# Four gate tiles of the delta projection computed inside the delta rule's first chunk

## The chip, the cores and the metric

The kernel runs on one core of a Trainium2 chip. The metric is the device time of one execution in microseconds (us); the kernel before takes 1758.41 us, the median of 3 runs (1757.74 to 1760.31). The engines of the core are TensorE (PE in the rows, its weight loads PEld), VectorE (DVE), ScalarE (ACT), GpSimd (POOL) and the queue that issues the transfers (SP). Each works through its own list of instructions in order, and they wait for one another by semaphores.

## What is computed

The reference is two transformer blocks on 256 tokens of width 1024: in the first, two kinds of attention and a layer of 16384 small experts; in the second, banded attention and then a gated delta rule, the mixer at which the change is made. 16 meta tokens stand in front there, so that it sees L = 272 tokens.

```
u = rms_norm(h, norm_w) @ w_in
qkv, z, b, a = split(u, [4096, 4096 + 2048, ... + 16])
qkv = silu(causal_depthwise_conv(qkv, conv_w))
q, k, v = split(qkv)                      # q, k l2-normed
beta = sigmoid(b)
g = -exp(a_log) * softplus(a + dt_bias)
o = chunked_gated_delta_rule(q, k, v, beta, g)
o = rms_norm(o, o_norm_w) * silu(z)
return o @ w_out
```

The gate z is needed only at the last step, when an output is multiplied by silu(z).

## The kernel before, in words

All weights come through a ring of four tiles of 128x1024 (512 KB each), loaded by SP in the order in which they are used. A weight tile is split in two: ScalarE rounds it to its high part (`make_high`, L177), and VectorE or GpSimd subtracts that from the tile for the low part (`make_low`, L189). Both parts have two buffers. TensorE multiplies a tile of the projection in 24 matmuls of 272 columns: 8 of the high part with the rounded input, 8 of the high part with the rest of the input, 8 of the low part (`tile_T`, L229 and L233). `tile_piece` (L272) does the same 24 matmuls in pieces, and is used so far to fill the attention stage.

**The projection** (`delta_in_stage`) has 49 tiles: 32 for the convolutions (c0 to c31; q, k, v), one for beta and the decays, 16 for the gate (z0 to z15). `mix_order` writes their order: a pair of convolution tiles and a gate tile in turn, with the tile of beta and the decays in the place of the first gate tile and one gate tile left over at the end. A convolution costs VectorE one multiplication and three multiply-adds (L1981, L1984) and ScalarE a Silu (L2047, or L2055 and L2056) and for q and k a square (L2051); it has three PSUM banks and two buffers of results, so that convolution i waits for the Silu of convolution i-2. A gate tile costs ScalarE one Silu out of PSUM (L2070). The low parts of the tiles with odd numbers are made by GpSimd from the third tile on, those with even ones by VectorE. Between the tiles stand matmuls that collect sums of squares (L1935, "gather") and spread the norms back (L1943, "spread", taken by VectorE in L2635, or L2640 and L2641). Steps on the decays are pinned to tile numbers t: at t=5 VectorE makes the doubled decays (L2009 to L2014), and at t=6 TensorE transposes them (L1960).

**The delta rule** (`delta_stage`) works through 5 chunks; chunk 0 holds the 16 meta tokens and has 3 levels of the inverse, the others have 5. Ahead of chunk 0 stand the decay sums and key products (`key_sums`, L2155 and L2157), the transposes of the keys (`turn_keys`, L2176) and values (`turn_values`, L2182), and `turn_m` (L2188), which needs the decays' exponentials and products of ScalarE and VectorE (L2563, L2396). Then each level has, for both halves b of the heads: `square` on TensorE (L2202), a copy by ScalarE (`take_power`, L2579), the product `grow` on TensorE (L2216), and an add on VectorE (`add_inverse`, L2427). The functions `beside` put the work of the next and the last chunk between these steps. A chunk ends with `solve` (L2225, L2230). PSUM banks 6 and 7 are unused in chunk 0. `store_out` multiplies the outputs of a chunk by the gate.

Both stages are blocks of their own: all engines meet between them. The four first tiles of the output weights (`dn_out`) are loaded at the start of the delta rule and split at its end.

Of the kernel before, what the change touches and what calls it, by code (L numbers as in the profile page):

```python
# [10 lines left out]
ACT = mybir.ActivationFunctionType  # L11
# [34 lines left out]
PAD = NCH * CH - L  # L46

# [47 lines left out]
def plan(k):  # L95
# [38 lines left out]
    for n in range(len(r.slots)):  # L134
        k.split.append(None if n in plain else n - sum(q < n for q in plain))
        engine = "gpsimd" if k.tiles["dn_in"] + AHEAD <= n < k.tiles["dn_out"] and n % 2 else "vector"
        made[engine] += n not in plain
        k.low_nth.append((engine, made[engine]))
# [1730 lines left out]
def mix_order():  # L1869


    out, z = [], 0
    for pair in range(DNK + DNV // 2):
        out += [("conv", 2 * pair), ("conv", 2 * pair + 1)]
        if pair == 0:
            out.append(("ba", 0))
        else:
            out.append(("z", z))
            z += 1
    return out + [("z", i) for i in range(z, DNV)]  # L1880


def delta_in_stage(k, unit, norm):
# [4 lines left out]
    first, order = k.tiles["dn_in"], mix_order()  # L1888
# [24 lines left out]
    with nc.Block() as block:  # L1913
# [58 lines left out]
        def _(dve):  # L1972
# [21 lines left out]
            for t in range(count):  # L1994
# [10 lines left out]
                if t + AHEAD < count and k.low_nth[first + t + AHEAD][0] == "vector":  # L2005
                    make_low(dve, k, first + t + AHEAD)
# [35 lines left out]
        def _(act):  # L2042
# [17 lines left out]
            for t in range(count + 1):  # L2060
                if t + AHEAD < count:
                    make_high(act, k, first + t + AHEAD)
# [32 lines left out]
def delta_stage(k):  # L2095
# [17 lines left out]
    rooted, normed, stored, chain, mean = k.start("d_rooted", "d_normed", "d_stored", "d_chain", "d_mean")  # L2113
    H = 4
# [25 lines left out]
    with nc.Block() as block:  # L2140
# [6 lines left out]
        def _(pe):  # L2147
            def key_sums(c):
# [155 lines left out]
            def beside(c, l, b):  # L2304

                if c + 1 < NCH:
# [24 lines left out]
            turn_keys(0, 0)  # L2331
            turn_m(0)
            turn_keys(0, 1)
# [27 lines left out]
        def _(dve):  # L2361
# [95 lines left out]
            def store_out(c):  # L2457
                dve.wait_ge(*oturn.at(c))
                for b in range(2):
# [36 lines left out]
            products(0)  # L2496
            key_rows(0, 1)
            value_rows(0, 0)
            value_rows(0, 1)
            for c in range(NCH):  # L2500
                first_inverse(c)
                if c + 1 < NCH:
                    spread_gates(c + 1)
                for l in range(1, levels(c) + 1):
                    for b in range(2):
                        beside(c, l, b)
                        add_inverse(c, l, b)
                if c:
# [41 lines left out]
        def _(act):  # L2550
# [30 lines left out]

            decays(0)
            take_turned(0)
            for c in range(NCH):
                for l in range(1, levels(c) + 1):
                    for b in range(2):
                        take_power(c, l, b)
                        if c + 1 < NCH and (l, b) == (2, 0):
# [500 lines left out]
```

## Time and profile before

| | us |
|---|---|
| median of 3 runs | 1758.41 |
| the profiled execution | 1757.97 |
| its span | 1756.2 |
| TensorE busy | 1665.5 (95%) |
| VectorE busy | 1188.5 (68%) |
| ScalarE busy | 896.0 (51%) |
| GpSimd busy | 71.1 (4%) |

A row of a timeline merges instructions of one line that follow each other: when the first started, how long they took to the end of the last, how many, and in brackets how long the engine had stood idle before and what ended that. In the trace a float32 matmul outside the tiles counts twice (the 16 of `square` as 32). The time from the start of one row to the start of the next is the pitch. The granted clock is that of TensorE, 1.00 for 2.4 GHz and 0.50 for 1.2 GHz.

### The profile page before, as it was taken

To read this page: it belongs to the slowest core of one execution; us is meant where nothing else is said; L and a number is where in the kernel's file an instruction comes from. 1 tells how busy PE (TensorE), PEld (TensorE's weight loads), DVE (VectorE), ACT (ScalarE), POOL (GpSimd) and SP (SyncE) were. 2 spreads that over 40 slices of the span, in tenths; PEclk is the share of its full clock that TensorE was granted. 3 is DMA by queue.
4 is the path that set the end of the run, shared out by engine and by line. 5 is a ranking of instruction groups with operands and counts; after the bars stand their busy time and mean duration, and the time that the engine had idled before them with its cause. 6 is when DMAs were issued, how large, how long until landed. Compare 5 with 4: busy or idle time off the path is not lost. (4 is left out here: it accounts for less than half of the span.)

```text
span 1756.2 us, 34029 instructions
## 1 busy us (share of the span) xinstructions
PE 1665.5 (95%) x13058; PEld 1469.2 (84%) x13058; DVE 1188.5 (68%) x2002; ACT 896.0 (51%) x1561; POOL 71.1 (4%) x35
## 2 busy tenths in 40 slices
PE   7989989999999999989999999987989999899989
PEld 7877788899999999988888888784667898788877
DVE  5556566689989799976666666654646656655565
ACT  4335544354554677756666666632645654233323
POOL 0000000100000000000000000000001333100000
PEclk9979999999999999999999999996999999999999
DMA  6533144555555444446666666540122445200004
GB/s 216 180 96 96 50 144 154 159 182 165 180 169 176 136 131 132 122 134 193 192 194 196 192 191 192 163 142 28 59 71 89 152 145 149 92 3 3 3 26 144
DMA packets 63221, 230.03 MB, mean 131 GB/s; under 512 B 7024, under 2 KB 7280, under 8 KB 63104
## 3 DMA queue, kind: packets, MB, share of 16 engines
q1 hardware_dynamic: 63104, 228.39, 41.5%
q8 instruction: 82, 1.34, 0.3%
q14 instruction: 35, 0.29, 0.0%
HBM read 227.32 MB, written 1.05 MB: 130 GB/s over the span
## 5 line engine op out<-in xcount | busy, mean ns | idle before, releaser
L1073 DVE TENSOR_TENSOR tile_low<-weights,tile_high 128x1024 fp32r<-128x1024 f32 x252 | 307.0, 1221 | 142.2 <-ACT tile_high L1063 138.6
L1063 ACT ACTIVATE tile_high<-weights 128x1024 fp32r<-128x1024 f32 x252 | 268.3, 1065 | 136.7 <-issue 136.7
L177 ACT ACTIVATE tile_high<-weights 128x1024 fp32r<-128x1024 f32 x169 | 178.2, 1057 | 250.6 <-issue 76.6
L189 DVE TENSOR_TENSOR tile_low<-weights,tile_high 128x1024 fp32r<-128x1024 f32 x146 | 178.0, 1223 | 167.6 <-ACT tile_high L177 149.8
L1125 PE MATMUL banks<-parts,tile_high 128*128 128x256 f32 x2048 | 269.9, 285 | 0.3 <-PEq L995 0.3
L1427 PE MATMUL banks<-tile_high,parts 128*128 128x512 f32 x1024 | 254.7, 391 | 4.7 <-ACT parts L1392 4.7
L1125 PEld LDWEIGHTS banks<-parts,tile_high 128*128 128x128 f32 x2048 | 254.2, 192 | 0.9 <-issue 0.9
L1427 PEld LDWEIGHTS banks<-tile_high,parts 128*128 128x128 f32 x1024 | 193.2, 189 | 45.1 <-issue 4.9
L229 PE MATMUL banks<-parts,tile_high 128*128 128x272 f32 (+1 forms) x1216 | 172.7, 296 | 4.2 <-PEq L464 3.4
L229 PEld LDWEIGHTS banks<-parts,tile_high 128*128 128x128 f32 x1216 | 159.3, 193 | 19.4 <-issue 16.8
L1130 PE MATMUL banks<-parts,tile_low 128*128 128x256 f32 x1024 | 145.4, 285 | 9.1 <-DVE tile_low L1073 9.1
L1130 PEld LDWEIGHTS banks<-parts,tile_low 128*128 128x128 f32 x1024 | 131.7, 192 | 12.3 <-DVE tile_low L1073 11.8
L1427 PE MATMUL banks<-tile_low,parts 128*128 128x512 f32 x512 | 137.3, 390 | 0.0
L1427 PEld LDWEIGHTS banks<-tile_low,parts 128*128 128x128 f32 x512 | 96.5, 189 | 20.2
L1179 ACT ACTIVATE big<-banks 128x256 f32 (+1 forms) x79 | 52.7, 667 | 117.7 <-PE banks L1130 117.7
L1200 ACT ACTIVATE rows<-rows,kept 128x128 f32<-128x128 f32 x256 | 79.9, 390 | 24.1 <-DVE rows L1281 23.9
L1392 ACT ACTIVATE parts<-big 128x256 fp32r (+1 forms) x128 | 87.8, 687 | 4.3 <-PEq L1106 4.3
L233 PE MATMUL banks<-parts,tile_low 128*128 128x272 f32 (+1 forms) x608 | 88.1, 287 | 0.0
L1445 DVE TENSOR_TENSOR parts<-big,parts 128x256 fp32r<-128x256 f32 x128 | 82.2, 644 | 1.0 <-ACT parts L1392 1.0
L2959 PE MATMUL banks<-tile_high,parts 128*128 128x512 f32 (+1 forms) x288 | 75.0, 407 | 7.6 <-ACT parts L2904 4.4
L233 PEld LDWEIGHTS banks<-parts,tile_low 128*128 128x128 f32 x608 | 80.8, 190 | 0.0
L1281 DVE TENSOR_TENSOR rows<-const,kept 128x1024 f32<-128x1024 f32 x64 | 76.5, 1218 | 0.1
(381 smaller groups left out, 2253.4 us busy)
## 6 DMA issues: line engine op xcount, KB each, us to landing
weights<-in_peer_u SPq DMA_DIRECT2D x128, 512.0 KB, 3.5
weights<-in_peer_v SPq DMA_DIRECT2D x128, 512.0 KB, 3.5
weights<-in_dn_in SPq DMA_DIRECT2D x49, 512.0 KB, 3.5
weights<-in_in_t SPq DMA_DIRECT2D x19, 512.0 KB, 3.6
weights<-in_attn_t SPq DMA_DIRECT2D x19, 512.0 KB, 3.6
weights<-in_in_m SPq DMA_DIRECT2D x16, 512.0 KB, 3.6
weights<-in_wq SPq DMA_DIRECT2D x16, 512.0 KB, 3.5
weights<-in_dn_out SPq DMA_DIRECT2D x16, 512.0 KB, 3.6
```

The costliest lines, as they stand in the source:

```text
L177: k.nc.scalar.activation(k.high[:, m % 2, :], k.ring.view(n), ACT.Copy).then_inc(*k.high_made.up())
L189: unit.tensor_tensor(k.low[:, m % 2, :], k.ring.view(n), k.high[:, m % 2, :].bitcast(F32), ALU.subtract).then_inc(*k.low_made[engine].up())
L229: ins = nc.tensor.matmul(out, high[:, c, :], rhs(c)[part], start=part + c == 0, stop=False)
L233: ins = nc.tensor.matmul(out, low[:, c, :], rhs(c)[0], start=False, stop=c == chunks - 1)
L1063: k.nc.scalar.activation(k.high[:, (s + j) % 2, :], k.ring.buf[:, j % RING, :], ACT.Copy).then_inc(k.high_made.sem, 1)
L1073: k.nc.vector.tensor_tensor(k.low[:, (s + j) % 2, :], k.ring.buf[:, j % RING, :], k.high[:, (s + j) % 2, :].bitcast(F32), ALU.subtract).th ...
L1125: ins = nc.tensor.matmul(ps[:, bank, 0:S], high[:, c, :], x[:, c, :], start=part + c == 0, stop=False)
L1130: ins = nc.tensor.matmul(ps[:, bank, 0:S], low[:, c, :], k.pair(S)[0][:, c, :], start=False, stop=c == KC - 1)
L1200: nc.scalar.activation(hot, hot, ACT.Copy, scale=k.chosenT[:, 2, Q * g + q:Q * g + q + 1]).then_inc(*scaled.up())
L1392: nc.scalar.activation(stage[:, j % STAGES, :], c_of(i, j), ACT.Copy).then_inc(staged.sem, 1)
L1427: ins = nc.tensor.matmul(ps[:, 2 * tt + half, :], c[:, j % STAGES, tt * P:tt * P + P], v[:, half, :], start=head and j + part == 0, stop=t ...
L1445: nc.vector.tensor_tensor(stage_low[:, j % STAGES, :], c_of(i, j), stage[:, j % STAGES, :].bitcast(F32), ALU.subtract).then_inc(staged_low ...
```

## The change

The last four gate tiles (z12 to z15) leave the projection, which keeps 45 tiles. The second, fourth and sixth pair of convolutions are no longer followed by a gate tile; from the seventh pair on each pair is. In the delta rule, late tile 0 is computed in one piece after the first transposes of the keys, and late tiles 1 to 3 in thirds of 8 matmuls between `turn_m` and the products of chunk 0, into banks 6 and 7. ScalarE copies the results out without Silu, in `take_z`, and applies one Silu to all four after the first half of chunk 1's fifth level. The high and low parts of late tile 0 are made at the end of the projection, those of the other three in the delta rule; all the late low parts are VectorE's. `store_out` waits for the late Silu.

```
-        else:
+        elif pair >= 6 or pair % 2 == 0:
             out.append(("z", z))
...
-    first, order = k.tiles["dn_in"], mix_order()
+    first, order = k.tiles["dn_in"], mix_order()[:-LATE_Z]
...
-                if t + AHEAD < count and k.low_nth[first + t + AHEAD][0] == "vector":
+                if t + AHEAD <= count and k.low_nth[first + t + AHEAD][0] == "vector":
                     make_low(dve, k, first + t + AHEAD)
...
-                if t + AHEAD < count:
+                if t + AHEAD <= count:
                     make_high(act, k, first + t + AHEAD)
...
+    z_pieces = {(0, 1, 0): ((1, 1),), (0, 1, 1): ((1, 2),), (0, 2, 0): ((2, 0), (2, 1)), (0, 2, 1): ((2, 2),),
+                (0, 3, 0): ((3, 0), (3, 1)), (0, 3, 1): ((3, 2),)}
+    z_taken, Z_LAST = {(0, 2, 0): 1, (0, 3, 0): 2, (0, 3, 1): 3}, (0, 2, 0)
...
             key_sums(0)
             turn_keys(0, 0)
+            late_z(0, 0, 1)
             turn_m(0)
+            late_z(1, 0, 3)
             turn_keys(0, 1)
...
             products(0)
+            make_low(dve, k, zfirst + 1)
             key_rows(0, 1)
...
                 first_inverse(c)
+                if c == 0:
+                    make_low(dve, k, zfirst + 2)
...
                         add_inverse(c, l, b)
+                        if (c, l, b) == Z_LAST:
+                            make_low(dve, k, zfirst + 3)
...
+            def take_z(i):
+                act.wait_ge(k.ring.used.sem, zfirst + i + 1)
+                nc.scalar.activation(k.z[:, DNV - LATE_Z + i, :], zbank(i), ACT.Copy).then_inc(*zcopied.up())
+
+            make_high(act, k, zfirst + 1)
             decays(0)
             take_turned(0)
+            take_z(0)
+            make_high(act, k, zfirst + 2)
...
                         take_power(c, l, b)
+                        if (c, l, b) in z_taken:
+                            take_z(z_taken[c, l, b])
+                        if (c, l, b) == Z_LAST:
+                            make_high(act, k, zfirst + 3)
+                        if (c, l, b) == (1, 5, 0):
+                            late = k.z[:, DNV - LATE_Z:DNV, :]
+                            act.wait_ge(*zcopied.at(LATE_Z))
+                            nc.scalar.activation(late, late, ACT.Silu).then_inc(*zopened.up())
```

In the changed file lines stand some way further on: `key_sums` is L2168 and L2170 there, `turn_keys` L2189, `turn_values` L2195, `turn_m` L2201, `square` L2215, `grow` L2229, `tile_piece` L273.

TensorE's list at the start of chunk 0, before:

```order
L2155 MATMUL banks<-big 128x512
L2157 MATMUL banks<-big 128x64 x8
L2176 MATMUL banks<-const,big 128x128 x4
L2188 MATMUL banks<-const,big 64x64 x16
L2176 MATMUL banks<-const,big 128x128 x4
L2182 MATMUL banks<-const,big 128x128 x8
L2202 MATMUL banks<-big 64x64 x32
L2216 MATMUL banks<-big 64x64 x8
L2202 MATMUL banks<-big 64x64 x16
L2155 MATMUL banks<-big 128x512
L2157 MATMUL banks<-big 128x64 x8
```

and of the changed kernel, from the same place:

```order
L2168 MATMUL banks<-big 128x512
L2170 MATMUL banks<-big 128x64 x8
L2189 MATMUL banks<-const,big 128x128 x4
L273 MATMUL banks<-parts,tile_high 128x272 x16
L273 MATMUL banks<-parts,tile_low 128x272 x8
L2201 MATMUL banks<-const,big 64x64 x16
L273 MATMUL banks<-parts,tile_high 128x272 x8
L2189 MATMUL banks<-const,big 128x128 x4
L2195 MATMUL banks<-const,big 128x128 x8
L2215 MATMUL banks<-big 64x64 x32
L273 MATMUL banks<-parts,tile_high 128x272 x8
L2229 MATMUL banks<-big 64x64 x8
```

Between the first transposes and the first product stand 40 matmuls of late tiles.

VectorE's list at t=4 (its end) to t=6 of the projection, before:

```order
L1984 SCALAR_TENSOR_TENSOR rows<-banks,param,rows 128x270 [waits conv_chain]
L1984 SCALAR_TENSOR_TENSOR rows<-banks,param,rows 128x269 [waits conv_chain]
L189 TENSOR_TENSOR tile_low<-weights,tile_high 128x1024 [waits tile_used,high_made]
L2009 SCALAR_TENSOR_TENSOR rows<-rows 16x272 [waits gate_act,tile_used]
L2010 TENSOR_SCALAR rows<-rows,small 16x272 [waits gate_vector]
L2012 COPY rows<-rows 48x2x16 [waits gate_cleared,gate_vector]
L2014 COPY rows<-rows 48x512 [waits gate_vector]
L1981 TENSOR_SCALAR rows<-banks,param 128x272 [waits conv_silu,tile_used,gate_vector]
```

and of the changed kernel:

```order
L1985 SCALAR_TENSOR_TENSOR rows<-banks,param,rows 128x269 [waits conv_chain]
L190 TENSOR_TENSOR tile_low<-weights,tile_high 128x1024 [waits tile_used,high_made]
L1982 TENSOR_SCALAR rows<-banks,param 128x272 [waits conv_silu,tile_used]
L1985 SCALAR_TENSOR_TENSOR rows<-banks,param,rows 128x271 [waits conv_chain]
L1985 SCALAR_TENSOR_TENSOR rows<-banks,param,rows 128x270 [waits conv_chain]
L1985 SCALAR_TENSOR_TENSOR rows<-banks,param,rows 128x269 [waits conv_chain]
L2010 SCALAR_TENSOR_TENSOR rows<-rows 16x272 [waits gate_act]
L2011 TENSOR_SCALAR rows<-rows,small 16x272 [waits gate_vector]
L2013 COPY rows<-rows 48x2x16 [waits gate_cleared,gate_vector]
```

A convolution (L1982, L1985), which waits for the Silu of an earlier one, now stands ahead of the decays (L2009 before, L2010 now).

ScalarE's list at the start of the delta rule, before:

```order
L2563 ACT_TABLE_LOAD
L2563 ACTIVATE big<-big 128x512
L2570 ACTIVATE big<-banks 128x4x128
L2579 ACTIVATE big<-banks 128x512 x3
L2563 ACTIVATE big<-big 128x512
L2566 ACTIVATE big<-big 128x512
```

and of the changed kernel (L178 makes a high part, L2586 is the Exp, L2593 takes the result of `turn_m`, L2602 is the copy of a power, L2607 that of a late tile):

```order
L178 ACTIVATE tile_high<-weights 128x1024
L2586 ACT_TABLE_LOAD
L2586 ACTIVATE big<-big 128x512
L2593 ACTIVATE big<-banks 128x4x128
L2607 ACTIVATE big<-banks 128x272
L178 ACTIVATE tile_high<-weights 128x1024
L2602 ACTIVATE big<-banks 128x512 x3
L2607 ACTIVATE big<-banks 128x272
L178 ACTIVATE tile_high<-weights 128x1024
L2586 ACTIVATE big<-big 128x512
L2589 ACTIVATE big<-big 128x512
```

Three high parts and the copies of the late tiles stand between the steps.

## Rows read from the trace of the kernel before

**Rows 1.** Windows: stretch, its us, busy us (instructions) by engine, granted clock, DMA share, GB/s.
```profile
1522.30:1530.90 8.60, 4.41 (x55) 3.59 (x54) 4.66 (x7) 2.31 (x3) 0.00 (x0) 1.00 0.67 244
1530.90:1537.70 6.80, 5.57 (x60) 4.79 (x60) 3.78 (x6) 1.09 (x2) 0.00 (x0) 0.50 0.01 2
1537.70:1549.90 12.20, 12.20 (x280) 11.35 (x278) 5.90 (x11) 4.20 (x9) 0.00 (x0) 1.00 0.01 3
```

**Rows 2.** Timeline, TensorE, handover and chunk 0: start, us, instruction, idle before and releaser.
```profile
1523.80 1.13 PE L2155 MATMUL banks<-big 128*128 128x512 f32 x2 [1.49 <-DVE big L2365]
...
1526.50 0.61 PE L2176 MATMUL banks<-const,big 128*128 128x128 f32 x4
1529.81 1.15 PE L2188 MATMUL banks<-const,big 64*64 64x64 f32 x32 [2.70 <-DVE big L2396]
1531.66 1.11 PE L2176 MATMUL banks<-const,big 128*128 128x128 f32 x4 [0.70 <-ACT big L2570]
...
1534.15 1.11 PE L2182 MATMUL banks<-const,big 128*128 128x128 f32 x4 [0.53 <-DVE rows L2382]
1535.19 3.21 PE L2202 MATMUL banks<-big 64*64 64x64 f32 x64
1538.24 0.63 PE L2216 MATMUL banks<-big 64*64 64x64 f32 x16
```

**Rows 3.** Timeline, TensorE, two projection tiles with nothing beside them.
```profile
1451.04 2.18 PE L229 MATMUL banks<-parts,tile_high 128*128 128x272 f32 x16
...
1454.06 2.18 PE L229 MATMUL banks<-parts,tile_high 128*128 128x272 f32 x16
```

**Rows 4.** Timeline, VectorE, the decays at t=5 of the projection.
```profile
1367.40 0.43 DVE L2009 SCALAR_TENSOR_TENSOR rows<-rows 16x272 f32<-16x272 f32 x1
...
1368.46 0.42 DVE L2014 COPY rows<-rows 48x512 f32<-48x512 f32 x1
```

**Rows 5.** Timeline, TensorE, the transposes at t=6 of the projection.
```profile
1370.61 0.51 PE L1960 MATMUL banks<-const,rows 48*128 48x48 f32 x5
```

**Rows 6.** Timeline, ScalarE, the Silu of convolution c2.
```profile
1367.42 0.43 ACT L2047 ACTIVATE big<-rows 128x272 f32<-128x272 f32 x1
```

**Rows 7.** Timeline, VectorE, the projection's end and chunk 0.
```profile
1515.50 0.50 DVE L1981 TENSOR_SCALAR rows<-banks,param 128x272 f32<-128x272 f32 x1 [1.05 <-PE banks L233]
...
1517.52 1.22 DVE L189 TENSOR_TENSOR tile_low<-weights,tile_high 128x1024 fp32r<-128x1024 f32 x1
...
1519.45 0.68 DVE L2641 TENSOR_TENSOR big<-banks,big 128x512 f32<-128x512 f32 x1
...
1532.81 0.69 DVE L2381 TENSOR_TENSOR big<-banks,kept 128x512 f32<-128x512 f32 x1 [3.06 <-PE banks L2176]
```

**Rows 8.** Timeline, ScalarE, the projection's end and the delta rule.
```profile
1514.55 1.06 ACT L177 ACTIVATE tile_high<-weights 128x1024 fp32r<-128x1024 f32 x1 [2.50 <-issue]
...
1522.35 0.40 ACT L2070 ACTIVATE big<-banks 128x272 f32<-128x272 f32 x1 [2.60 <-PE banks L233]
1523.02 1.28 ACT L2563 ACT_TABLE_LOAD   x1 [0.27 <-PEq L1913]
...
1531.00 0.60 ACT L2570 ACTIVATE big<-banks 128x512 f32<-128x512 f32 x1 [3.95 <-PE banks L2188]
...
1575.20 0.39 ACT L2579 ACTIVATE big<-banks 128x256 f32<-128x256 f32 x1 [1.28 <-PE banks L2202]
...
1592.78 0.63 ACT L2563 ACTIVATE big<-big 128x512 f32<-128x512 f32 x1 [2.51 <-DVE big L2373]
```

**Rows 9.** Timeline, TensorE, a filler piece of 12 matmuls in the attention stage.
```profile
1236.35 1.78 PE L272 MATMUL banks<-parts,tile_high 128*128 128x272 f32 x12
1238.06 1.51 PE L1624 MATMUL banks<-big 16*64 16x128 f32 x8
```

**Rows 10.** Timeline, TensorE, solve of chunk 0 and last product of chunk 1.
```profile
1550.47 1.98 PE L2225 MATMUL banks<-big 64*64 64x128 f32 x32 [0.52 <-DVE big L2427]
...
1579.05 0.68 PE L2216 MATMUL banks<-big 64*64 64x64 f32 x16
```

More of the change, by code:

```diff
@@ L46 @@
 PAD = NCH * CH - L
+LATE_Z = 4
 class Signal:
@@ L135, in plan @@
         k.split.append(None if n in plain else n - sum(q < n for q in plain))
-        engine = "gpsimd" if k.tiles["dn_in"] + AHEAD <= n < k.tiles["dn_out"] and n % 2 else "vector"
+        engine = "gpsimd" if k.tiles["dn_in"] + AHEAD <= n < k.tiles["dn_out"] - LATE_Z and n % 2 else "vector"
         made[engine] += n not in plain
@@ L2113, in delta_stage @@
     rooted, normed, stored, chain, mean = k.start("d_rooted", "d_normed", "d_stored", "d_chain", "d_mean")
+    zcopied, zopened = k.start("d_late_z_copied", "d_late_z_opened")
+    zfirst = k.tiles["dn_out"] - LATE_Z
+    zhigh, zlow = k.pair(L)
+    zbank = lambda i: ps[:, 6 + i % 2, 0:L]
+    z_pieces = {(0, 1, 0): ((1, 1),), (0, 1, 1): ((1, 2),), (0, 2, 0): ((2, 0), (2, 1)), (0, 2, 1): ((2, 2),),
+                (0, 3, 0): ((3, 0), (3, 1)), (0, 3, 1): ((3, 2),)}
+    z_taken, Z_LAST = {(0, 2, 0): 1, (0, 3, 0): 2, (0, 3, 1): 3}, (0, 2, 0)
     H = 4
@@ L2147, in _, with late_z @@
         def _(pe):
+            def late_z(i, piece, pieces):
+                if i >= 2 and piece == 0:
+                    pe.wait_ge(*zcopied.at(i - 1))
+                tile_piece(pe, k, zfirst + i, zbank(i), lambda c: (zhigh[:, c, :], zlow[:, c, :]), piece, pieces)
             def key_sums(c):
@@ L2304, in beside @@
             def beside(c, l, b):
+                for i, piece in z_pieces.get((c, l, b), ()):
+                    late_z(i, piece, 3)
                 if c + 1 < NCH:
@@ L2458, in store_out @@
                 dve.wait_ge(*oturn.at(c))
+                dve.wait_ge(*zopened.at(1))
                 for b in range(2):
```

## The prediction

> **What bounds the kernel now.** TensorE is busy nearly everywhere, so moving work gains only where TensorE stands idle or runs at its lower clock. Read first the windows by stage [rows 1]. In the 8.6 us from the end of the delta projection, TensorE works for 4.41 us only; in the next 6.8 us it works for 5.57 us at a granted clock of 0.50, which is 1.2 GHz; in the 12.2 us after that it is busy throughout, at 1.00. Then read TensorE's own rows [rows 2]: it waits 1.49 us for the first step of the delta rule, 2.70 us for the decays and their products (before turn_m, L2188), 0.70 and 0.53 us before transposes. The clock was 1.00 until the long wait ended and then fell to 0.50 [rows 1]; at 0.50 four transposes take 1.11 us against 0.61 us at 1.00, and the first two squares 3.21 us [rows 2]. From the first product (L2216, 1538.24) to the last product of chunk 0 nothing waits: every round trip through ScalarE and VectorE lies under other TensorE work. So the start of chunk 0 has room, its inverse steps have none.
>
> **What leaves the projection.** Four gate tiles of 24 matmuls. A tile with nothing beside it has a pitch of 3.02 us (1454.06 - 1451.04) [rows 3]. The one-off matmuls between tiles (gather, spread, the gate's sums) stay and each still breaks one tile, so four plain tiles go: 4 x 3.02 = **-12.1 us**.
>
> **What the closer convolutions cost.** The tile after c3 (t=5) was a gate tile and is now convolution c4. VectorE makes the doubled decays at t=5 in 1.48 us, 1367.40 to 1368.88 [rows 4], and TensorE's transposes at t=6 need them; TensorE reaches these at 1370.61 [rows 5]. Now the convolution is queued ahead of them. It shares its buffer with c2, whose Silu ran only from 1367.42 to 1367.85 [rows 6]. So it starts at 1367.9 and ends at 1369.95 (2.05 us: a convolution that starts at 1515.50 is followed by the next step at 1517.52 [rows 7]); the decays take until 1371.45, the transposes start at 1371.5: **+0.9 us**, where before it was nothing. Bounds: 0 (if VectorE comes through sooner) and 1.2. The later steps pinned to a tile number, t=8, 10, 11, 12 and 14, also have convolutions before them; by the same durations VectorE is behind by 1 us at most, and a low part is needed only 2 us into its tile, so nothing. From the seventh pair on, the order is the old one, three tiles earlier.
>
> **The end of the projection.** VectorE now makes the low part of the first late tile after the last convolution, with one gate tile to follow instead of two. Before, the last engine to finish was ScalarE at 1522.75 [rows 8], 0.44 us after TensorE (1523.80 - 1.49 = 1522.31) [rows 2]. Now, from the point X where the last convolution's tile is done: backlog 0.1, convolution 2.0, low part 1.15 to the next start, two spreads of 0.7, to X+4.75 [rows 7]; TensorE has a spread and a tile left and ends at X+3.85. VectorE ends 0.9 us after TensorE instead of ScalarE's 0.44: **+0.45 us** on the handover. Bounds 0 and 0.8.
>
> **The start of chunk 0, on the old clock, aligned at VectorE's first instruction.** Sums and first transposes as before, until 1527.1 [rows 2]. Late tile 0 comes in one piece: 24 matmuls, 3.0 us, and the price of breaking in. In the attention stage 12 such matmuls between others take 1.71 us (1238.06 - 1236.35) [rows 9], where half a plain tile takes 1.51. So **0.2 us for each piece**; bounds 0 and 0.4. It ends at 1530.25; turn_m could start at 1529.81, so it is 0.45 us late. ScalarE began to take the result 1.19 us after turn_m's start, and needed 0.60 [rows 2, 8]: 1532.05. Meanwhile 8 matmuls of tile 1 (1.0 us and the break) run on TensorE, to 1532.35. Transposes at full clock, 0.6 each: 1532.95 and 1533.5. VectorE's two key rows take 1.34 us from their start to the release of TensorE (1532.81 to 1534.15) [rows 2, 7]: 1533.0 to 1534.35. The last transposes run to 1534.95, the first square (half of two, at twice the speed) to 1535.95. VectorE scales the last values and starts the inverse by 1536.35, ScalarE copies the power by 1536.95, TensorE meanwhile does the second square and the next 8 matmuls of tile 1, until 1538.1. The first product starts at 1538.1, against 1538.24: **-0.1 us**, with 40 of the 96 moved matmuls done. They took the place of the long wait and of the half clock.
>
> Of the queues moved past: ScalarE's first high part (1.06 us) stands ahead of the first Exp, and the Exp's table load (1.28 us) stands before its wait for VectorE already [rows 8]; both end by 1525.4, while the Exp's argument takes the sums (1523.80 and 1.13 us) and two VectorE steps, 1526.3. The low parts (1.22 us each) fall on VectorE while another engine is ahead of it: after the products (1529.75 to 1531.0, next needed 1533.0), after the inverse's start (to 1537.5), after the third add. The late tiles land while the projection still runs, since their four slots come free at its last four tiles; the four output-weight loads now wait for the late low parts, some 27 us later, but over 100 us before chunk 4 wants them. All of this costs nothing.
>
> **The inverse steps.** Here TensorE has no gap, so the remaining 56 matmuls cost their time: 56 x 0.126 = 7.0 us, and five pieces at 0.2: **+8.0 us**. The only wait at the end of chunk 0, 0.52 us for VectorE's last add before solve [rows 10], stays, since no piece stands behind that add. The one Silu over four tiles, at chunk 1's fifth level, costs a load of 1.28 and, at 0.60 for 512 columns, some 1.2 us: after the copy that ended at 1575.6 ScalarE has until about 1578.6, with the last product at 1579.05 [rows 8, 10] and one earlier copy of 0.4 still to make; it fits. The next Exp needs its table again; it stood idle 2.51 us for VectorE [rows 8], and the load of 1.28 goes under that. Both cost nothing; uncovered they would be 2.5 and 1.3.
>
> **Sum.** -12.1 + 0.9 + 0.45 - 0.1 + 8.0 = **-2.85 us**. The profiled execution took 1757.97 us (a span of 1756.2 and 1.8 around it), 0.44 under the median, and would become 1755.1, with a span of 1753.35; the median of 1758.41 becomes **1755.5 us**. A measurement of this kernel can tell about 0.2%, or 3.5 us, from no change: the forecast is just inside that, and "faster" begins at 1754.9.
>
> **Rivals.** *More than that (A2).* The +0.9 is a schedule by hand; the 0.2 per piece comes from a stage with other neighbours, and chunk 0 changes between shapes at each step already. With no stall at t=6 and 0.1 per inner piece: -2.85 - 0.9 - 0.5 = -4.25, which is 1754.2. For it: between the decays' end and the transposes there were 1.7 us to spare before. Against: the late Silu of c2 is in the trace.
>
> *The clock falls all the same (B).* After the wait of 2.70 us the clock fell to 0.50 for 6.8 us, after the 1.49 us at the handover it did not [rows 1, 2]. That wait grows to 1.94, between the two. If it falls in there, late tile 0 runs at 1.2 GHz; squares and transposes took 1.5 to 1.8 times as long at it [rows 2], so 3.4 to 6.8 us of it lose 1.4 to 2.8 us: 1756.9 to 1758.3. The Trainium skill, "TensorE: Matmul & The Clock Gate", Part 1, says that idleness drops TensorE to 1.2 GHz, that sustained work restores it, and that the point of the change varies from run to run; by that rule the handover could go either way, and the trace agrees in so far as the longer wait dropped the clock and the shorter did not.
>
> *The moved work comes back in full (C).* If late tile 0 only pushes turn_m and all behind it, the 40 matmuls cost 5.0 + 0.6 too: -12.1 + 0.9 + 0.45 + 5.6 + 8.0 = +2.85, 1761.3. Against: the 2.70 us are really empty [rows 2].
>
> *Slower (D): ScalarE and VectorE become the bound of chunk 0.* Each inverse step is square, copy, product, add. ScalarE gets 3 x 1.06 + 4 x 0.40 = 4.8 us and VectorE 3 x 1.22 = 3.7 us more [rows 7, 8], in order, ahead of copies and adds. If all of it lay on the path: +8.5 - 2.85 = +5.65, 1764.1. It decides from the point where what stands ahead of a copy exceeds the TensorE work between a square and its product, which the pieces themselves raise by 1.2 to 2.2 us; the worst place has 1.46 us (a copy and the last high part) under 5 us of it. Against: all the slacks above.
>
> **How the numbers follow.** Forecast 0.45, of which 0.10 falls beyond 1754.9; A2 0.22; B 0.20; C 0.06; D 0.07. Faster by over 0.2%: 0.10 + 0.22 = 0.32. Slower by over 0.2% (above 1761.9): D and a bit of C, 0.08. Within: 0.60. The range goes from 1752.8 (A2, its five inner pieces at nothing, and the handover's 0.45 and some spread gone) to B's upper end with half a microsecond of spread, 1758.8; it leaves out D, C and some of A2.
>
> **What the profile after would show.** No long idle before turn_m; the granted clock at 1.00 from the projection's end through chunk 0; the first product 15.0 us after VectorE's first instruction of the stage; solve 7.9 us later than before on that clock; an idle of about 0.9 us before the transposes at t=6, and 1.9 us before the first sums. The forecast is wrong if a piece costs much more than its matmuls and 0.2 us, if copies wait behind high parts, or if the clock drops.

## The result, and the profile after

The changed kernel takes 1761.8 us (median of 21 runs, 1760.64 to 1773.17), the kernel before 1758.88 (21 runs, 1757.26 to 1760.78). The ratio is 1.0022, 95% interval 1.0015 to 1.0028: **0.22% slower, +2.9 us**, where -2.85 was forecast. The forecast and its range (to 1758.8) were wrong, and by 5.8 us in the middle.

The head of the page shows little: TensorE is busy 8.8 us longer (1665.5 before), which here means slower, since the matmuls are the same.

```profile
span 1765.0 us, 34032 instructions
...
PE 1674.3 (95%) x13058; PEld 1475.7 (84%) x13058; DVE 1193.6 (68%) x2004; ACT 899.8 (51%) x1564; POOL 66.8 (4%) x33
```

So I cut both traces at the same instructions of TensorE. Each column is from one profiled execution; "projection" is from the first tile to the last matmul of a tile, "handover" the idle time to the first key sum, "product" the first `grow`, "solve" that of chunk 0:

| us | before | after | forecast of the difference | measured |
|---|---|---|---|---|
| projection | 175.04 | 168.18 | -12.1 + 0.9 | -6.86 |
| handover | 1.49 | 1.90 | +0.45 | +0.41 |
| first key sum to first product | 14.44 | 18.98 | -0.1 | +4.54 |
| first product to solve | 12.23 | 20.31 | +8.0 | +8.08 |
| solve to the output projection | 157.59 | 157.61 | 0 | +0.02 |
| output projection to the end | 48.14 | 48.14 | 0 | 0 |

The profiled execution of after, 1766.81 us, is one of the slowest: 2.64 us of its span are lost ahead of the projection, where nothing is changed and the clock was at 0.50 for 7 us more in all (among others 10.3 us instead of 6.8 from 1294.7 on). Two stages are off: the projection by 4.3 us and the start of chunk 0 by 4.6.

**The projection.** TensorE at t=6 and at the first spread, where [rows 5] shows transposes without a wait:

```profile
1372.73 0.63 PE L1936 MATMUL banks<-rows,big 128*16 128x272 f32 x2
1375.81 0.51 PE L1961 MATMUL banks<-const,rows 48*128 48x48 f32 x5 [2.45 <-DVE rows L2015]
1376.25 3.69 PE L230 MATMUL banks<-parts,tile_high 128*128 128x272 f32 x16
1379.74 1.31 PE L234 MATMUL banks<-parts,tile_low 128*128 128x272 f32 x8
1380.98 0.63 PE L1936 MATMUL banks<-rows,big 128*16 128x272 f32 x2
...
1455.96 0.72 PE L1944 MATMUL banks<-rows,const 16*128 16x272 f32 x2 [1.04 <-DVE rows L1504]
```

VectorE, which it waits for, after:

```profile
1371.19 1.57 DVE L1985 SCALAR_TENSOR_TENSOR rows<-banks,param,rows 128x271 f32<-128x271 f32 x3
1372.79 1.92 DVE L2010 SCALAR_TENSOR_TENSOR rows<-rows 16x272 f32<-16x272 f32 x1
...
1452.12 0.43 DVE L1498 TENSOR_TENSOR rows<-rows 16x272 f32<-16x272 f32 x1
1452.59 2.53 DVE L1500 TENSOR_TENSOR rows<-rows 16x272 f32<-16x272 f32 x1
```

and GpSimd:

```profile
1372.05 2.37 POOL L190 TENSOR_TENSOR tile_low<-weights,tile_high 128x1024 fp32r<-128x1024 f32 x1 [7.17 <-ACT tile_high L178]
...
1452.12 2.69 POOL L190 TENSOR_TENSOR tile_low<-weights,tile_high 128x1024 fp32r<-128x1024 f32 x1 [3.64 <-ACT tile_high L178]
```

The first step on the decays, 0.43 us before [rows 4], took 1.92, and the step L1500, like L1498 a step of 0.43 in the Newton iteration that makes the norms' roots, took 2.53. Each ended 0.29 and 0.31 us after GpSimd's low part beside it had ended (1374.42, 1454.81): it stood still until then. In the trace of before it came half a microsecond behind the decays, which ended at 1368.88 [rows 4]. GpSimd's row there:

```profile
1369.35 2.39 POOL L189 TENSOR_TENSOR tile_low<-weights,tile_high 128x1024 fp32r<-128x1024 f32 x1 [7.17 <-ACT tile_high L177]
```

My own working had moved them to 1369.95, right under it, and I did not look at GpSimd's row. The Newton iteration of before even shows such a hold, which I had overlooked, beside a low part that ended at 1453.81:

```profile
1451.42 2.39 POOL L189 TENSOR_TENSOR tile_low<-weights,tile_high 128x1024 fp32r<-128x1024 f32 x1 [3.63 <-ACT tile_high L177]
...
1453.24 0.87 DVE L1497 TENSOR_TENSOR rows<-rows 16x272 f32<-16x272 f32 x1
```

This is the step that took 0.43 us in after (L1498); here it ended 0.30 us behind GpSimd. After the wait of 2.45 us a tile of after has a pitch of 4.73 us (1380.98 - 1376.25) instead of 3.21 (the same tile at full clock, 1376.18 - 1372.97 in the first run below): the clock had fallen too.

**The start of chunk 0.** TensorE after; compare [rows 2]:

```profile
1519.99 2.07 PE L2168 MATMUL banks<-big 128*128 128x512 f32 x2 [1.90 <-DVE big L2382]
1521.85 3.51 PE L2170 MATMUL banks<-big 128*128 128x64 f32 x16
1525.16 1.06 PE L2189 MATMUL banks<-const,big 128*128 128x128 f32 x4
1525.87 3.98 PE L273 MATMUL banks<-parts,tile_high 128*128 128x272 f32 x16
1529.65 1.44 PE L273 MATMUL banks<-parts,tile_low 128*128 128x272 f32 x8
1531.01 1.15 PE L2201 MATMUL banks<-const,big 64*64 64x64 f32 x32
...
1535.18 0.66 PE L2195 MATMUL banks<-const,big 128*128 128x128 f32 x4 [0.94 <-DVE rows L2399]
...
1537.78 1.26 PE L273 MATMUL banks<-parts,tile_high 128*128 128x272 f32 x8
1538.97 0.68 PE L2229 MATMUL banks<-big 64*64 64x64 f32 x16
```

and the windows of after (columns as in [rows 1]); the granted clock stands behind the busy times:

```profile
1372.70:1376.60 3.90, 1.45 (x10) 0.85 (x10) 3.69 (x7) 1.80 (x4) 1.72 (x1) 1.00 0.35 96
1376.60:1380.10 3.50, 3.50 (x18) 3.50 (x17) 2.36 (x4) 0.07 (x1) 0.00 (x0) 0.51 0.22 89
...
1520.00:1530.20 10.20, 10.20 (x41) 9.17 (x42) 5.10 (x7) 2.26 (x3) 0.00 (x0) 0.50 0.17 53
1530.20:1540.00 9.80, 8.86 (x165) 8.02 (x166) 5.21 (x8) 3.03 (x5) 0.00 (x0) 1.00 0.25 66
```

The clock fell to 0.50 (1.2 GHz) as the wait of 1.90 us ended, and stayed there for 10.2 us of unbroken work: key sums, transposes and nearly all of late tile 0. It is the lower of the two levels: the four transposes took 1.06 us instead of 0.61 [rows 2]. The long wait before `turn_m` is gone, as meant.

### The profile page after: what moved, and what is told of

Same layout as the page of the kernel before. It is cut to its first block and busy times, and to the rows that moved or that the text cites. A ratio compares the mean times of both kernels' runs of the same rounds, so it can differ in the third digit from the quotient of the medians.

```text
span 1765.0 us, 34032 instructions
## 1 busy us (share of the span) xinstructions
PE 1674.3 (95%) x13058; PEld 1475.7 (84%) x13058; DVE 1193.6 (68%) x2004; ACT 899.8 (51%) x1564; POOL 66.8 (4%) x33
## 3 DMA queue, kind: packets, MB, share of 16 engines
HBM read 227.32 MB, written 1.05 MB: 129 GB/s over the span
## 5 line engine op out<-in xcount | busy, mean ns | idle before, releaser
L178 ACT ACTIVATE tile_high<-weights 128x1024 fp32r<-128x1024 f32 x169 | 178.2, 1057 | 247.3 <-issue 71.5
L1126 PEld LDWEIGHTS banks<-parts,tile_high 128*128 128x128 f32 x2048 | 255.2, 192 | 0.9 <-issue 0.9
L230 PE MATMUL banks<-parts,tile_high 128*128 128x272 f32 (+1 forms) x1152 | 164.3, 296 | 4.2 <-PEq L465 3.4
L230 PEld LDWEIGHTS banks<-parts,tile_high 128*128 128x128 f32 x1152 | 151.0, 193 | 19.8 <-issue 16.9
L234 PE MATMUL banks<-parts,tile_low 128*128 128x272 f32 (+1 forms) x576 | 84.0, 288 | 0.0
```

Of the source, the lines that this page charges most:

```text
L178: k.nc.scalar.activation(k.high[:, m % 2, :], k.ring.view(n), ACT.Copy).then_inc(*k.high_made.up())
L230: ins = nc.tensor.matmul(out, high[:, c, :], rhs(c)[part], start=part + c == 0, stop=False)
L234: ins = nc.tensor.matmul(out, low[:, c, :], rhs(c)[0], start=False, stop=c == chunks - 1)
L1126: ins = nc.tensor.matmul(ps[:, bank, 0:S], high[:, c, :], x[:, c, :], start=part + c == 0, stop=False)
```

## The experiments

Two theories stood for the two stages. *Port*: GpSimd's low part holds VectorE's small steps; against it, *order*: the convolution in front is alone to blame. *Clock*: the wait of 1.90 us drops the clock at the handover; against it, *pieces*: late tile 0 is slow for where it stands. All edits are against the changed kernel, where nothing else is said.

### The low part beside the decays made by VectorE

```
-        engine = "gpsimd" if ... and n % 2 else "vector"
+        engine = "gpsimd" if ... and n % 2 and n != k.tiles["dn_in"] + 7 else "vector"
...
-                if t + AHEAD <= count and ...
+                if t != 5 and t + AHEAD <= count and ...
                     make_low(dve, k, first + t + AHEAD)
...
+                    make_low(dve, k, first + 7)      # behind the decays, in the block of t == 5
```

> The changed kernel, with one low part (tile 7 of the projection) made by VectorE behind the decays at t=5 instead of by GpSimd. In the changed kernel's trace the first of the decays (16x272) took 1.92 us where it takes 0.43 us in the kernel before, and ended 0.3 us after a GpSimd low part (1372.05 to 1374.42). Theory port: a VectorE instruction that reads two operands from SBUF stands still while GpSimd makes a low part. Then the decays take 1.5 us again, TensorE's wait before the transposes falls from 2.45 to about 1.0 us (what the prediction's queue alone gives), and the kernel gains 1.5 us, or 3 us if the shorter wait also keeps the clock up. Theory queue: the decays are late only for the convolution and its late Silu; GpSimd doesn't matter; the wait stays near 2.45 us or grows, the time stays at 1761.8.

Measured: 1758.53 us, ratio to before 0.9998 (0.9989 to 1.0007); 3.3 us less than the changed kernel. VectorE and then TensorE:

```profile
1371.00 0.43 DVE L2010 SCALAR_TENSOR_TENSOR rows<-rows 16x272 f32<-16x272 f32 x1
```

```profile
1372.53 0.51 PE L1961 MATMUL banks<-const,rows 48*128 48x48 f32 x5 [0.95 <-DVE rows L2015]
1372.97 2.28 PE L230 MATMUL banks<-parts,tile_high 128*128 128x272 f32 x16
...
1376.18 0.63 PE L1936 MATMUL banks<-rows,big 128*16 128x272 f32 x2
```

The step is back at 0.43 us with the convolution still in front: *port* holds. The wait is 0.95 us where +0.9 was forecast: that working was right but for GpSimd. No clock fell at t=6, and the projection took 165.10 us. At the handover the same wait of 1.90 us left the clock at 1.00, and the first product came after 14.20 us. But a stretch of 3.4 us at 0.50 stood later, in the delta rule at 1617.1, and solve to output projection took 159.24 us, 1.6 more.

### The decays ahead of the convolution

```
             for t in range(count):
+                if t == 5:
+                    (the steps on the decays, moved here from behind the low part)
```

> The changed kernel, with the decays at t=5 ahead of the convolution on VectorE. Both theories: the decays end before TensorE reaches the transposes, the wait of 2.45 us is gone, and with it the half clock that follows it (tile 7 had a pitch of 4.73 us instead of 3.19). If that half clock is in most executions, the gain is 2.45 + 1.5 = 4.0 us (1757.8); if it is in the profiled one alone, 2.45 us (1759.3).

Measured: 1764.41 us, 1.0037 (1.0023 to 1.0051). The order mends the wait fully (no idle time before the transposes, the projection 164.14 us, 4.0 less), and the kernel is 2.6 us slower than the changed one in the median (each of its 6 runs is above 17 of the 21), where 2.5 to 4.0 us less was expected. The trace has 0.50 from 1515.1 to 1521.9, at the handover (17.43 us to the first product), and behind solve 0.50 for 3.4 us from 1658.5 and for 10.3 from 1692.6, where the changed kernel has one stretch of 3.4 (162.41 us instead of 157.61). So in the two profiled executions 4.0 us are won in the projection, 1.6 up to the first product, and 4.8 lost behind solve. That the median moved the other way, the one trace of each can't explain in full.

### A few matmuls in the handover's wait

```
+            pe.wait_ge(*conv.at(30))
+            keep_busy(k, 2, 1)
```

stand behind the projection's last tile. The call issues one float32 matmul of 384 columns on constants, which the trace counts as two; it is called the two matmuls below. It takes 0.8 us inside the wait.

> The changed kernel, with one dummy float32 matmul of 384 columns (0.69 us by the rows of the kernel before) on TensorE at the end of the projection, in the time in which it waits for VectorE. Theory clock: the wait of 1.90 us at the handover drops the clock (0.50 for 10.2 us in the profiled execution); with 1.2 us of wait, less than the 1.49 us after which it stayed up before, it stays at 1.00 and the first product comes 15.0 us after VectorE's first instruction instead of 19.7: a gain of up to 4.7 us where the drop would have come, 1.5 to 2 in the median. Rival: the drop has another cause (then it stays, and the time is 1761.8 within 0.5).

Measured: 1760.85 us, 1.0016 (1.0007 to 1.0024). TensorE here:

```profile
1517.78 0.81 PE L284 MATMUL banks<-const 128*128 128x384 f32 x2
1519.84 1.13 PE L2170 MATMUL banks<-big 128*128 128x512 f32 x2 [1.25 <-DVE big L2384]
...
1522.89 2.25 PE L273 MATMUL banks<-parts,tile_high 128*128 128x272 f32 x16
1524.97 1.16 PE L273 MATMUL banks<-parts,tile_low 128*128 128x272 f32 x8
1526.07 1.15 PE L2203 MATMUL banks<-const,big 64*64 64x64 f32 x32
```

The key sums start no sooner, and everything behind them up to the first product runs at full clock: late tile 0 has a pitch of 3.18 us (1526.07 - 1522.89) against 5.14 in the changed kernel (1531.01 - 1525.87), and the first product comes after 14.19 us instead of 18.98. That is *clock*, not *pieces*. Again a stretch of 3.4 us at 0.50 appeared at 1622.1 (159.22 us behind solve). The median fell by 1.0 us only, where 1.5 to 2 was expected, and its interval overlaps that of the changed kernel.

### The low part beside the Newton step made by VectorE

```
+        ... and n % 2 and n != k.tiles["dn_in"] + 29 else "vector"
```

> The changed kernel, with the low part of tile 29 of the projection made by VectorE instead of GpSimd. In the changed kernel one step of the Newton iteration (16x272, two operands) took 2.53 us instead of 0.43, while GpSimd made that low part, and TensorE waited 1.04 us for it. Theory port: the step takes 0.43 us again; TensorE's wait of 1.04 us is gone; a gain of 1.0 us (1760.8). Theory order: the iteration is late because a low part now stands ahead of it on VectorE; then the wait stays or grows with the 1.2 us more on VectorE.

Measured: 1763.36 us, 1.0023 (1.0013 to 1.0033). VectorE, then TensorE:

```profile
1451.91 0.43 DVE L1500 TENSOR_TENSOR rows<-rows 16x272 f32<-16x272 f32 x1
```

```profile
1454.17 0.72 PE L1944 MATMUL banks<-rows,const 16*128 16x272 f32 x2
```

2.53 us became 0.43 and the wait of 1.04 is gone: *port* a second time, and the projection is 1.1 us shorter. The total did not follow: 1760.8 was expected, and the median is 1.6 us above the changed kernel's (the intervals overlap), with the clock at 0.50 for 6.8 us at the handover.

### The kernel before with its long wait filled

```
             turn_keys(0, 0)
+            keep_busy(k, 6, 3)
             turn_m(0)
```

in the kernel before: three matmuls on constants, six in the trace, where the change puts late tile 0.

> The kernel before, with three dummy float32 matmuls of 384 columns (2.1 us) on TensorE in the wait of 2.70 us before turn_m; nothing is moved. Theory clock: the half clock of 6.8 us at the start of chunk 0 is gone, and from the first key sum to the first product it takes 13.0 us instead of 14.4, 1.4 less (by the rows at 1.00 for transposes and squares). That would be the part of the change's gain that needs no moved work. Rival: the clock falls there all the same, at the handover's 1.49 us or in the waits left; then 14.4 or more, and no gain.

Measured: 1759.87 us against 1758.71, 1.0003 (0.9994 to 1.0012): no gain. TensorE, and a window of it:

```profile
1529.33 2.10 PE L283 MATMUL banks<-const 128*128 128x384 f32 x6
1532.20 1.15 PE L2188 MATMUL banks<-const,big 64*64 64x64 f32 x32 [0.77 <-DVE big L2397]
```

```profile
1618.60:1622.00 3.40, 3.40 (x34) 3.07 (x32) 1.51 (x6) 0.57 (x1) 0.00 (x0) 0.50 0.00 0
```

The first product came 12.63 us after the key sums instead of 14.44: the half clock of [rows 1] was the long wait's, and filling the wait removes it. The 1.8 us were lost again at 1618.6, in a stretch that ran at full clock in the kernel before (159.28 against 157.59 behind solve).

### One late tile only

```
-LATE_Z = 4
+LATE_Z = 1
...
-        elif pair >= 6 or pair % 2 == 0:
+        else:
             out.append(("z", z))
```

and no pieces, copies and parts of late tiles 1 to 3: the projection keeps its old order and loses one gate tile, and nothing stands between the inverse steps.

> One late gate tile only, the last one, whole, ahead of turn_m; the order of the projection stays that of the kernel before. Theory (port and order spoil the projection, the gap at the start of chunk 0 is a true gap, the inverse steps have none): the projection is 3.0 us shorter, no new wait in it; handover 1.9 instead of 1.49; key sum to first product 12.9 to 13.2 instead of 14.4 at full clock; first product to solve 12.2 as before. Together -4.0 us (1754.8), or -2 if the handover drops the clock. Rival: moving even one tile costs what it saves (turn_m is held up by it): 1758.

Measured: 1755.17 us, 0.9983 (0.9974 to 0.9992). TensorE:

```profile
1520.65 1.13 PE L2166 MATMUL banks<-big 128*128 128x512 f32 x2 [1.90 <-DVE big L2379]
...
1523.71 2.25 PE L273 MATMUL banks<-parts,tile_high 128*128 128x272 f32 x16
1525.79 1.16 PE L273 MATMUL banks<-parts,tile_low 128*128 128x272 f32 x8
1526.88 1.15 PE L2199 MATMUL banks<-const,big 64*64 64x64 f32 x32
...
1533.50 0.68 PE L2227 MATMUL banks<-big 64*64 64x64 f32 x16
```

The tile lies wholly in the long wait: 172.02 us of projection (-3.02), 12.85 to the first product (-1.6), 12.28 to solve (nothing). The clock did not fall behind this wait of 1.90 us.

### The changed kernel with all three mended, and without the matmuls

Four late tiles, the decays first, low part 29 on VectorE, the two matmuls in the handover:

> The changed kernel with all four late tiles, the decays ahead of the convolution at t=5, tile 29's low part on VectorE, and one dummy matmul (0.69 us) at the end of the projection. The sum of the prediction without its +0.9: projection 163.1 us long (175.0 before), first key sum to first product 14.2, first product to solve 20.3 (12.2 before), handover 1.9: -3.7 us, 1755.1, if the clock stays up at the handover and in the later chunks as before; 2 to 5 us more if it falls, as in two of the four experiments before, which lost up to 4.8 us behind solve although nothing is changed there.

Measured: 1755.47 us, 0.9982 (0.9973 to 0.9991). The same without `keep_busy`:

> The kernel with all three repairs (1755.47 us) less the one dummy matmul at the end of the projection. The instructions that do work are the same; TensorE waits 1.9 us at the handover instead of 1.25 after the dummy. Theory clock: the longer wait drops the clock at the handover in most executions (0.50 for 3.4 to 10.2 us, first key sum to first product 16 to 19 us instead of 14.2) and may shift a drop into the later chunks: 1758 to 1762. Rival: the dummy does nothing and the repairs of the projection alone give the gain: 1755.5 within 0.7, first key sum to first product 14.2.

Measured: 1759.10 us against 1759.12, 0.9997 (0.9988 to 1.0006). This is the pair that isolates the clock. The medians are 3.6 us apart, and 3.2 when each is taken against the kernel before of its own measurement (the two were made on two chips); the intervals of the ratios overlap at their ends, but every run of the one is below every run of the other. A window of the kernel with them:

```profile
1513.00:1523.00 10.00, 9.06 (x96) 8.39 (x95) 6.79 (x10) 3.37 (x5) 0.00 (x0) 1.00 0.31 98
```

and without them:

```profile
1515.10:1522.00 6.90, 6.90 (x33) 6.90 (x33) 4.63 (x7) 0.67 (x2) 0.00 (x0) 0.51 0.07 26
```

TensorE without them, at the same place:

```profile
1513.47 1.13 PE L2168 MATMUL banks<-big 128*128 128x512 f32 x2 [1.90 <-DVE big L2382]
...
1530.82 0.68 PE L2229 MATMUL banks<-big 64*64 64x64 f32 x16
```

17.35 us from key sum to product (1530.82 - 1513.47) against 14.21 with them: 3.1 us, nearly all of it. The mended kernel's stages are 162.98, 1.90, 14.21, 20.32 and 157.64: with the two stalls and the fallen clock gone, the change gives -3.7 us in the stages and -3.2 in the median.

### Three late tiles, two forms

Both have `LATE_Z = 3` and no late tile 3; they differ in the pairs that have no gate tile. The first leaves out the last scaling of one head's keys (`finish(15)`, some 0.7 us of VectorE at the projection's end), for which its order has no place, and that step is missing from its work:

```
-        elif pair >= 6 or pair % 2 == 0:
+        elif pair not in (5, 7):
```

> Three late tiles, and the two gate tiles left out of the order are those of the sixth and the eighth pair, so that nothing changes up to t=14 and GpSimd keeps the same half of the low parts. Theory: no wait before the transposes at t=6 and none before the first spread, with the decays and the iteration where they were: projection 9.1 us shorter (166.0), handover 1.9, key sum to first product 14.2, first product to solve 4.6 us longer (16.8). Together -4.3 us, 1754.5, or 1756 to 1757 if the handover drops the clock. Rival (late tiles cost in the projection whatever the order): a wait of 1 us or more appears elsewhere in it.

Measured: 1755.77 us, 0.9982 (0.9973 to 0.9991). The first spread waits 1.2 us for the Newton step, as the rival in the expectation said, and its handover is another one: the last spread stands in it, with a wait of 1.07 us behind. The second has `pair not in (5, 6)` and the two matmuls in the handover:

> Three late tiles with the gate tiles of the sixth and seventh pair left out of the order (all steps of the projection kept, the iteration at an odd tile as in the kernel before), and the dummy matmul. Theory: no new wait in the projection, which lasts 166.0 us (175.0 less three tiles), no wait of 1 us before the first spread; first key sum to first product 14.2, first product to solve 16.6: -4.5 us and a bit for the clock, 1754.3. Rival: the wait before the first spread appears here too (1.0 us) and the gain is 3.5.

Measured: 1759.45 us, 1.0000 (0.9991 to 1.0009). Up to solve it did what was expected of it: no wait of a microsecond in the projection (165.98 us), 14.21, 16.62. Behind solve it took 162.26 us instead of 157.6, and the total missed the expected 1754.3 by 5.1 us. Two windows of it:

```profile
1615.20:1618.60 3.40, 3.26 (x32) 3.26 (x32) 2.15 (x9) 0.00 (x0) 0.00 (x0) 0.50 0.00 0
1656.10:1666.40 10.30, 10.30 (x117) 9.52 (x114) 3.04 (x7) 2.65 (x3) 0.00 (x0) 0.50 0.01 2
```

TensorE there:

```profile
1655.12 2.78 PE L2239 MATMUL banks<-big 64*64 64x128 f32 x32 [2.01 <-DVE big L2445]
```

and the same instructions in the mended kernel with four late tiles:

```profile
1652.02 1.98 PE L2240 MATMUL banks<-big 64*64 64x128 f32 x32 [2.01 <-DVE big L2446]
```

The same wait of 2.01 us ends both times, with the same work ahead of it; in one kernel the clock falls behind it, in the other it does not. What tells the two apart is not in their instructions there.

### One late tile and the two matmuls

> One late tile and the dummy matmul at the end of the projection. Projection 172.0, first key sum to first product 12.85, first product to solve 12.3 as without the dummy. Theory clock: without the dummy the clock may fall at the handover in some executions (its times spread from 1753.4 to 1756.6); with it fewer do, 1754.5. Rival: the spread comes from the drops before the projection and behind chunk 0, which the dummy doesn't touch: 1755.2.

Measured: 1754.65 us against 1759.12, **0.9974 (0.9965 to 0.9983)**: 4.5 us under the kernel before, the fastest version found. The stages are 172.03, 1.90, 12.85, 12.28 and 157.61. Against the kernel with one late tile and no such matmuls nothing is gained that can be told (1755.17, the intervals overlap), since there the clock had not fallen.

## Why the prediction was wrong, point by point

- **Four plain tiles, -12.1: right.** With the stalls gone the projection took 162.98 us instead of 175.04, -12.06.
- **The closer convolutions, +0.9: the step that failed first.** The durations were right (0.95 us of wait with the low part away from GpSimd). Missing was that the decays, once moved to 1369.95, lie on GpSimd's low part, so that a step of 0.43 us takes 1.92 and the wait is 2.45: +1.55. "Bounds 0 and 1.2" took every duration as fixed; before's own trace spoke against it, with the Newton step shown above (0.87 us instead of 0.43) and with L2028 (one input, 128x40 elements, in 2.16 us beside a low part from 1389.55 to 1391.95).
- **"The later steps ... so nothing": wrong by 1.04 us.** I followed the pinned steps up to t=14 and not the Newton step, which moves against the odd tiles of GpSimd when tiles ahead of it leave.
- The Trainium skill, "SBUF — State Buffer", section "Who interferes with whom", has the rule that I had not weighed: a VectorE instruction with two inputs in SBUF contends with a GpSimd instruction that reads SBUF, and the loser stands fully blocked until the other has finished. The trace agrees: both slow steps, and L1497 of before, have two inputs in SBUF and ended 0.3 us after GpSimd's; by that rule, on before's rows, GpSimd ends at 1371.74, the first step 0.3 us later, the other three 1.05 us after that, and the wait at t=6 comes out at 2.5 us (1373.1 - 1370.61). The convolutions, with one input in PSUM, run beside the same low part in their usual time (1.57 us at 1371.19).
- **The clock behind that wait: not in the prediction at all.** Rival B looked for the clock at the handover only. A wait that the change creates in the middle of a stage can drop it too: one tile with a pitch of 4.73 instead of 3.21, +1.5 us.
- **The handover, +0.45: right** (1.90 instead of 1.49, +0.41), though with a slip: the terms of VectorE's path add up to X+4.65 and not X+4.75, which gives +0.35.
- **The start of chunk 0: the working was right at full clock, the clock was not.** Where the clock stayed up the first product came 14.20 us after the key sums, against 14.44 before: -0.24, where the sum had -0.1. The wait inside it was foreseen as well: VectorE's key rows keep TensorE for 0.94 us, and the working has 0.85 (1533.5 to 1534.35). The clock is rival B, with too small a chance (0.20) and too small a price (1.4 to 2.8): of six profiled kernels with a handover of 1.9 us and nothing in it, four fell (the changed one for 10.2 us, three for 6.8 or 6.9) and two did not, and the four lost 4.8 and some 3.2 us. In four kernels with the two matmuls none fell. The mistake of price was the length, taken from the one drop in [rows 1].
- **The inverse steps, +8.0: right** (+8.08), and so is the 0.2 us for a piece: eight matmuls between others have a pitch of 1.19 us (1538.97 - 1537.78), of which 1.01 are their own. No copy and no add waited for a late part: rival D was not seen. Rival C was not either: in the kernel with one late tile the long wait took a whole tile and gave 1.6 us back besides.
- **Nothing behind solve: right** for the changed kernel (+0.02), and luck, as the experiments showed.

**The account.** From -2.85 to +2.9 are 5.8 us: 1.55 and 1.04 for the blocked steps, 1.5 for the clock behind the first of them, and 1.7 are left for the clock at the handover. In the profiled execution it cost 4.8. The timed executions have no stages, but six kernels give an estimate of what it costs in the median. Take the changed kernel's stages with 14.21 us for the first product (410.3 from the first tile to the end), and another kernel's stages and the difference of the two medians: what is missing is 1.8, 1.4, 2.5, 0.5, 1.2 and 0.7 us (low part 7, decays first, matmuls, low part 29, all mended, all but the matmuls), if what lies ahead of the projection costs all alike. So the four causes are shown, and their sizes in the profiled executions; that the handover's share of the median is 1.7 us is an estimate, with 0.5 to 2.5 about it, and how often the clock falls there in an execution that is not profiled stays open.

**What the change could be worth.** Late tile 0 fills an empty wait and is all of the gain (-4.1 us in the stages, -3.5 and -4.5 in two medians). Late tiles 1 to 3 save 9.05 us in the projection and cost 1.35 ahead of the first product and 8.04 behind it, together 9.4: nothing, or a little less than nothing, and they bring the stalls. The prediction had both numbers (three tiles at 3.02, and 8.0) and added them up without asking whether the second to fourth tile pay for themselves.

## What to carry to other kernels

Price a moved piece of work for itself: the first tile, which fell into an empty wait, was worth 4 us, and the next three, cut into pieces between busy steps, nothing. When a change shifts small VectorE steps against GpSimd's instructions, lay both timelines over each other, since a step of 0.4 us that has two inputs in SBUF takes all that is left of GpSimd's. And a wait of two microseconds on TensorE can have two prices, its own and that of the clock behind it; a few matmuls on constants inside it can save the second, but only a comparison of whole kernels shows whether the drop has gone or has moved.

## What the runs showed of the hardware

The stretches at 0.50 from the projection on, in the profiled execution of each kernel (in brackets TensorE's wait just before it, for those spoken of above):

| kernel | median | at 0.50 (us of the span) |
|---|---|---|
| before | 1758.88 | 1530.9-1537.7 (wait 2.70), 1687.9-1691.3 |
| after | 1761.8 | 1376.6-1380.1 (2.45), 1520.0-1530.2 (1.90), 1697.5-1700.9 |
| low part 7 | 1758.53 | 1617.1-1620.5, 1688.8-1692.2 |
| decays first | 1764.41 | 1515.1-1521.9 (1.90), 1658.5-1661.9, 1692.6-1702.9 |
| matmuls in the handover | 1760.85 | 1376.4-1379.8, 1622.1-1625.5, 1693.8-1697.2 |
| low part 29 | 1763.36 | 1375.8-1379.2, 1519.2-1526.0 (1.90), 1693.3-1696.7 |
| before, filled | 1759.87 | 1618.6-1622.0, 1690.2-1693.7 |
| one late tile | 1755.17 | 1683.9-1687.4 |
| all mended | 1755.47 | 1684.6-1688.0 |
| three late tiles, pairs 5 and 7 | 1755.77 | 1685.1-1688.5 |
| all mended but the matmuls | 1759.10 | 1515.1-1522.0 (1.90), 1689.2-1692.6 |
| one late tile and matmuls | 1754.65 | 1684.4-1687.8 |
| three late tiles and matmuls | 1759.45 | 1615.2-1618.6, 1656.1-1666.4 (2.01) |

All the stretches behind solve follow one kind of wait: chunks 2, 3 and 4 each end with waits of 1.1 and 2.0 us ahead of their solve, in all thirteen kernels, and each of these stretches begins between 0.1 us before and 1.1 us after such a wait of 2.0 us ends. Behind that of chunk 4 the clock fell in twelve kernels, behind that of chunk 2 in four, behind that of chunk 3 in two.

Unexpected was how much of every result this is. The kernels with one stretch of 3.4 us are the four fastest, all within 1.2 us, though they differ by three gate tiles in where the work is done (one of them leaves out a step, see above). Waits of 1.9 to 2.0 us drop the clock in some kernels and not in others, in the same place with the same work ahead, and filling a wait earlier can bring a drop 85 us later (filled kernel before: 1.8 us won, 1.7 lost). The Trainium skill, "TensorE: Matmul & The Clock Gate", Part 1, says that the point at which the clock changes varies; here the medians of 6 to 21 runs largely kept the order that single profiles showed, which speaks for drops that fall much alike in each execution of one kernel and shift with an edit ahead of them; that was not tested by itself. Which of several equal waits the clock falls behind was not settled.

GpSimd pays for the contention as well, where VectorE's instruction with two inputs did not start after it. In the changed kernel its low part of 1452.12, which starts with VectorE's step of 0.43 us, took 2.69 us, and those of 1396.27 and 1460.10, which start while VectorE makes a low part (from 1395.60 and 1459.96), took 2.79 and 3.34; in the kernel before one took 3.43 in the same way (1457.46, behind 1457.42). All others in these two projections took 2.37 to 2.41.
